# One core, hybrid encoder block with 32 experts: the last expert's part added to the stored output by an indirect DMA, experts 30 and 31 in turn, down weights issued in order of use

## The chip, the cores and the metric

One NeuronCore of a Trainium2 chip runs the whole program. Five engines work side by side, each on its own list of instructions, and meet only at semaphores: PE (matmul), DVE (VectorE), ACT (ScalarE), POOL (GpSimd) and SP (SyncE, which here does nothing but issue DMAs). Sixteen DMA engines move data; the DMAs that SP issues form one queue, those of ACT and of POOL others. The metric is the device time of one execution in microseconds (us), smaller is better. It holds a little more than the span of the profile: for the profiled execution of the kernel before, 1085.68 us against a span of 1083.8 us.

## What is computed

512 tokens of width 1024 go through one layer: two attention-like branches, their mixing, and then a mixture of 32 experts with 8 per group. The change lies wholly in the experts' part:

```python
def hier_moe(h, w_rg, b_rg, w_re, b_re, w_gate, w_up, w_down):
    """Top-1 expert group, then top-2 SwiGLU experts inside that group."""
    ...
    gates = jnp.einsum('tk,tke->te', top_w, jax.nn.one_hot(expert_ids, N_EXPERTS, dtype=f32))
    y = jnp.zeros((B * S, D), f32)
    for e in range(N_EXPERTS):
        hid = jax.nn.silu(t @ w_gate[e]) * (t @ w_up[e])
        y = y + gates[:, e:e + 1] * (hid @ w_down[e]).astype(f32)
    return y.reshape(B, S, D)
...
        x = x + hier_moe(h2, ...).astype(dt)
    return x
```

All inputs and the output are float32. Each token goes to two experts, so that an expert has 32 tokens on average.

## The kernel before

The kernel gives every expert 48 slots in a block of 64 rows (`SLOTS`, `WIDE`), and two experts share the 128 partitions as a pair. The pair's tokens are gathered from DRAM by an indirect DMA on POOL's queue (L2254), transposed on PE (L1093) and evicted by DVE. Should an expert have more than 48 tokens, a loop behind the last expert runs once more for each further block; in the runs here it has no round (`n_more` is 0), though every engine loads `n_more` and branches over the loop.

**One expert on PE.** `product(e)` multiplies with the gate and up weights (L1106, 32 matmuls, two pieces of 2 MB), ACT applies SiLU (L1510), DVE multiplies with the up half into `hid` (L2021), PE transposes it (L1112), ACT copies the result into `hidT` (L1514), and `down_of(e)` multiplies with the down weights (L1122, 16 matmuls, one piece of 2 MB). ACT (L1505) and DVE (L2014) split the sum `y` into a high and a low part, each fp32r. When both experts of a pair are there, `combine` brings the rows back to their tokens: for each of eight tiles of 128 tokens x 512 columns a matmul of a one-hot matrix `pick` (made by DVE, L2008) with the high part (L1128) and one with the low part (L1129), after which DVE adds the tile to `x2` (L1996). The eight tiles of a pair are spread over the next two experts, four each, with three PSUM banks in rotation, so that a tile waits until DVE has added the one three tiles before it.

**Weights.** All expert weights come by SP's queue, in the order that SP issues them. Gate and up pieces, numbered u = 2e and 2e + 1 (W60 and W61 are those of expert 30, W62 and W63 those of expert 31), go round through a ring of seven places, the down pieces (D30 is that of expert 30; D31 comes in two halves) through three. SP waits until PE has freed a place and issues the next load into it. In the loop over e it issues W(2e+1), W(2e+2) and then D(e), although the order of use is W(2e), W(2e+1), D(e), W(2e+2).

**The end.** PE runs `product(30)`, four tiles of pair 14, the transposes, `product(31)`, four tiles, the transposes, and then both down products one behind the other (L1122, 32 matmuls). Expert 31 has banks of its own (4 and 7) and its own `hidT_last`, so that nothing waits between the two. Then `combine_last` makes the eight tiles of the last pair. For two of them PE first copies `x2` into the bank by a matmul with the identity (L1149), and ACT evicts and stores them (L1559, L1561); the other six DVE adds (L1996), and SP stores each as it is done (L630). The last instructions (L118) are the meeting of all engines at the program's end.

Of the kernel before, what the change touches and what calls it, by code (L numbers as in the profile page):

```python
# [64 lines left out]
def encoder_block(nc, x, norm1_g, w_in, gla_w_a2, gla_b_a, gla_norm_g, dsa_q_norm_g, dsa_k_norm_g,  # L65
# [38 lines left out]
    outd = out[0].rearrange("(t p) d -> p t d", p=P)  # L104
    wind = w_in[0].rearrange("(k p) n -> p k n", p=P)
# [12 lines left out]
    with ExitStack() as ctx:  # L118
# [120 lines left out]
        def product_bank(e):  # L239
            return bank[{1: 6, NE - 1: 4}.get(e, 0)]  # L240

        def y_bank(e):
            return bank[{1: 3, NE - 1: 7}.get(e, 1)]
# [4 lines left out]
        def up_half(e):  # L248
# [10 lines left out]
        m_pick = [piece_r(0, 512, 512 * hf) for hf in range(2)]  # L259
# [16 lines left out]
        hidT, hidT_last = [columns.rearrange("p (c h s) -> p c h s", c=2, h=2)  # L276
                           for columns in (bias[3][:, 256:512], piece(5, words=256))]

        def hidT_of(e):
            return hidT_last if e == NE - 1 else hidT  # L280

# [48 lines left out]
        tok_more = sb("tok_more", [P, 2])  # L330
# [13 lines left out]
            m_w m_idx m_xg m_pick m_comb m_added wdn_last  # L344
# [81 lines left out]
        COPIED = {3: 0, TILES - 1: 4}  # L426
        ADDED = [j for j in range(TILES) if j not in COPIED]

        def last_added(j):

            return TILES * (PAIRS_E - 1) + ADDED.index(j) + 1

# [11 lines left out]
        def combined_in(e):  # L444


            p, q = divmod(e, 2)
            if p == 0:
                return [], []
            tiles = list(range(TILES * (p - 1), TILES * p))[T * q:T * q + T]  # L450
            ahead = 3 if q and e < NE - 1 else 4
            return tiles[:ahead], tiles[ahead:]
# [26 lines left out]
        def _(sp):  # L479
# [113 lines left out]
            for e in range(4, NE):  # L593
                sp.wait_ge(s["gu_part"], e)
                load(2 * e + 1)
                if e < NE - 1:
                    sp.wait_ge(s["gu_ready"], e - 2)
                    load(2 * e + 2)
# [3 lines left out]
                if e < NE - 2:  # L602
                    sp.wait_ge(s["y_ready"], e - 2)
                    if e == 4:
                        load_down_half(4, 0)
                    else:
                        load_down(e)
# [19 lines left out]
            for j in ADDED:  # L627
                hf, t = divmod(j, T)
                sp.wait_ge(s["x_added"], last_added(j))
                sp.dma_start(outd[:, t, hf * BLK:(hf + 1) * BLK], x2[:, t, hf * BLK:(hf + 1) * BLK])\  # L630
                    .then_inc(s["out_stored"], 16)
# [4 lines left out]
        def _(pe):  # L636
# [506 lines left out]
            def combine_last():  # L1143

                p = PAIRS_E - 1
                pe.wait_ge(s["x_added"], TILES * p)
                for j, b in COPIED.items():
                    hf, t = divmod(j, T)
                    mm(bank[b][:, :], ident[:, :], x2[:, t, hf * BLK:(hf + 1) * BLK], start=True, stop=False)  # L1149
                for j in range(TILES):  # L1150
                    hf, t = divmod(j, T)
                    if t == 0:
                        pe.wait_ge(s["pick_ready"], 2 * p + hf + 1)
                        pe.wait_ge(s["y_lo_ready"], 4 * p + 4 if hf else 4 * p + 3)
                    b = COPIED[j] if j in COPIED else COMB_BANKS[ADDED.index(j) % 3]
                    if j not in COPIED and ADDED.index(j) >= 3:
                        pe.wait_ge(s["x_added"], last_added(ADDED[ADDED.index(j) - 3]))
                    cols = slice(t * P, (t + 1) * P)
                    mm(bank[b][:, :], pick[hf][:, cols], y_hi[p % 2][hf], start=j not in COPIED, stop=False)
                    mm(bank[b][:, :], pick[hf][:, cols], y_lo[p % 2][hf], start=False, stop=True)\  # L1160
                        .then_inc(s["comb_ps"], 1)
# [17 lines left out]
            def down_of(e):  # L1179
# [4 lines left out]
                down(y_bank(e), [wdn_half(e, h) for h in range(2)], e % 2, s["y_ready"], hidT_of(e),  # L1184
# [18 lines left out]
            for e in (NE - 2, NE - 1):  # L1203
                front, _ = combined_in(e)
                product(e)
                combine(front)
                if e == NE - 1:
                    pe.wait_ge(s["hidT_ready"], e)
                transposes_of(e)
            down_of(NE - 2)  # L1210
            down_of(NE - 1)

            n_more = pe.value_load(own_i[0:1, MORE:MORE + 1], min_val=0, max_val=MORE)
            with pe.If(n_more > 0):
                pe.wait_ge(s["x_added"], TILES * (PAIRS_E - 1))
                pe.wait_ge(s["y_lo_ready"], 2 * NE)
                with pe.Fori(0, n_more) as t:
# [7 lines left out]
                    pe.wait_ge(s["hidT_ready"], t + (NE + 1))  # L1225
                    down(bank[1], [wdn[0][:, h] for h in range(2)], 0, s["y_ready"])
                    pe.wait_ge(s["y_lo_ready"], t * 2 + (2 * NE + 2))
                    pe.wait_ge(s["m_pick"], t * 2 + 2)
                    for j in range(TILES):
                        hf, i = divmod(j, T)  # L1230
                        if j >= 3:
                            pe.wait_ge(s["m_added"], t * TILES + (j - 2))
                        combine_tile(bank[COMB_BANKS[j % 3]][:, :], m_pick[hf], y_hi[0][hf], y_lo[0][hf], i, s["m_comb"])
                    pe.wait_ge(s["m_added"], t * TILES + TILES)
            combine_last()
# [3 lines left out]
        def _(act):  # L1239
# [272 lines left out]
            def evict_hidT(e):  # L1512
                act.wait_ge(s["hidT_ps"], e + 1)
                A(hidT_of(e), bank[5][:, 0:HALF].rearrange("p (c h s) -> p c h s", c=2, h=2), ACT.Copy)\  # L1514
# [16 lines left out]
            for e in (NE - 2, NE - 1):  # L1531
                silu(e)
                evict_hidT(e)
            for e in (NE - 2, NE - 1):
                evict_y(e)

            n_more = act.value_load(own_i[0:1, MORE:MORE + 1], min_val=0, max_val=MORE)
            with act.If(n_more > 0):
                act.wait_ge(s["comb_ps"], TILES * (PAIRS_E - 1))
                with act.Fori(0, n_more) as t:  # L1540
# [12 lines left out]
                    high_parts(bank[1], 0, 0, s["y_hi_ready"])  # L1553


            for i, (j, b) in enumerate(COPIED.items()):
                hf, t = divmod(j, T)
                act.wait_ge(s["comb_ps"], TILES * (PAIRS_E - 1) + j + 1)
                A(x2[:, t, hf * BLK:(hf + 1) * BLK], bank[b][:, :], ACT.Copy).then_inc(s["act_s"], 1)  # L1559
                act.wait_ge(s["act_s"], 2 * T + i + 1)  # L1560
                act.dma_start(outd[:, t, hf * BLK:(hf + 1) * BLK], x2[:, t, hf * BLK:(hf + 1) * BLK])\  # L1561
                    .then_inc(s["out_stored"], 16)
            act.wait_ge(s["out_stored"], 16 * TILES)


        @block.vector
        def _(dve):
# [377 lines left out]
            st.did(V.memset(tok_more[:, :], float(S)))  # L1945
# [71 lines left out]
            def gated(e):  # L2017
                dve.wait_ge(s["silu_ready"], e + 1)
                if e in (1, NE - 1):
# [16 lines left out]
            pick_tokens(0)  # L2036
            for e in range(2, NE - 2):
# [12 lines left out]
            for e in (NE - 2, NE - 1):  # L2050
                front, _ = combined_in(e)
                add_combined(front[:1])
                gated(e)
                add_combined(front[1:])
# [272 lines left out]
```

## Time and profile before

| | us |
|---|---|
| median of 3 runs | 1085.6 |
| lowest and highest | 1085.42 and 1088.79 |
| profiled execution | 1085.68 |
| its span | 1083.8 |
| granted TensorE clock, mean | 0.997 of full speed |

| engine | busy us | share of the span |
|---|---|---|
| PE | 1056.9 | 98% |
| DVE | 545.2 | 50% |
| ACT | 343.6 | 32% |
| POOL | 290.4 | 27% |

The experts take the span from about 634 us on. PE's busy share cannot say by itself what bounds this stretch, since the DMA engines are as full as PE is. Two things tell more: the chain of work that ended last, with the stretches in which PE waits for something the profile does not name ("issue"), and the time from each DMA's issue to its landing, which gives the moment at which each piece of weights is there. The stretch behind the last weight is read from the timeline.

### The profile page before, as it was taken

What the parts mean: (1) busy time and instruction counts of PE and PEld (TensorE: products, weight loads), DVE (VectorE), ACT (ScalarE), POOL (GpSimd) and SP (SyncE); (2) the same over time, 40 slices, a digit from 0 to 9 for tenths busy, and PEclk for the clock granted to TensorE, in tenths of its full rate; (3) what the DMA queues carried; (4) which work ended last, traced back from release to release, by engine and by line L of the source; (5) the groups of instructions that cost most, each with busy time, mean ns of one, the idle gap of its engine ahead of it and who ended that gap; (6) DMA issues with size and microseconds to landing.
All of it is one profiled execution on the core that took longest, in us unless ns stands there. A gap on an engine that the chain in (4) does not pass through costs nothing.

```text
span 1083.8 us, 13000 instructions
## 1 busy us (share of the span) xinstructions
PE 1056.9 (98%) x5078; PEld 689.7 (64%) x5078; DVE 545.2 (50%) x1030; ACT 343.6 (32%) x620; POOL 290.4 (27%) x197
## 2 busy tenths in 40 slices
PE   7999999999999999999999999999999999998998
PEld 6777888777788888888888853444444444443443
DVE  4533895699850432239993363333333333333334
ACT  6356632445442555541233311111111111111111
POOL 6733344455552544443423010000000000000000
PEclk9999999999999999999999999999999999999999
DMA  8613333224051322244459989999999999999995
GB/s 214 162 40 78 78 78 78 60 78 117 21 141 37 75 78 59 59 161 133 115 195 380 330 348 426 425 428 426 425 428 426 427 427 425 425 426 429 428 427 209
DMA packets 117598, 263.39 MB, mean 243 GB/s; under 512 B 11808, under 2 KB 97824, under 8 KB 104224
## 3 DMA queue, kind: packets, MB, share of 16 engines
q1 hardware_dynamic: 113792, 255.75, 63.0%
q0 software_dynamic: 2352, 4.18, 1.1%
q10 hardware_dynamic: 1392, 2.62, 0.6%
q8 instruction: 41, 0.67, 0.3%
q14 instruction: 21, 0.17, 0.0%
HBM read 262.33 MB, written 4.20 MB: 246 GB/s over the span
## 4 chain that ended last, share of the span: by engine, by line
PE 95%; issue 2%; DMA 1%; DVE 1%; ACT 0%; SPq 0%; DVEq 0%; ACTq 0%
PE bank L1106 20%; PE bank L653 19%; PE bank L672 14%; PE bank L1122 11%; PE bank L908 8%; PE bank L999 4%; PE bank L1128 3%; PE bank L1129 2%; PE bank L880 2%; PE bank L863 2%; PE bank L1093 1%; PE bank L1112 1%; PE bank L871 1%; PE bank L748 1%; PE bank L810 1%
## 5 line engine op out<-in xcount | busy, mean ns | idle before, releaser
L2138 POOL TENSOR_TENSOR piece_r<-arena,piece_r 128x1024 fp32r<-128x1024 f32 x84 | 203.0, 2424 | 240.5 <-ACT piece_r L1267 240.2
L1106 PE MATMUL bank<-arena,work 128*64 128x512 f32 x1024 | 225.5, 592 | 0.0
L653 PE MATMUL bank<-piece_r 128*128 128x512 f32 (+1 forms) x936 | 218.6, 389 | 0.0
L653 PEld LDWEIGHTS bank<-piece_r 128*128 128x128 f32 x936 | 172.5, 188 | 35.9 <-issue 3.5
L1106 PEld LDWEIGHTS bank<-arena,work 128*64 128x64 f32 x1024 | 77.5, 137 | 140.6 <-issue 140.5
L1996 DVE TENSOR_TENSOR arena<-bank,arena 128x512 f32<-128x512 f32 x126 | 81.9, 683 | 165.4 <-PE bank L1129 165.0
L672 PE MATMUL bank<-piece_r 128*128 128x512 f32 x672 | 155.9, 391 | 0.5 <-ACT piece_r L1267 0.5
L672 PEld LDWEIGHTS bank<-piece_r 128*128 128x128 f32 x672 | 125.3, 188 | 29.2 <-issue 3.5
L1267 ACT ACTIVATE piece_r<-arena 128x1024 fp32r<-128x1024 f32 x83 | 87.5, 1058 | 97.3 <-DMA arena<-w_branch_gla_in 49.8
L2254 POOL DMA_INDIRECT arena<-x_rows,idx_pair x15 | 15.2, 1010 | 329.4 <-PE bank L1093 313.6
L2014 DVE TENSOR_TENSOR piece_r<-bank,piece_r 64x512 fp32r<-64x512 f32 x64 | 44.1, 688 | 98.5 <-ACT piece_r L1505 97.5
L908 PE MATMUL bank<-piece_r 128*128 128x512 f32 x384 | 87.6, 390 | 0.0
L1122 PE MATMUL bank<-arena,bias 128*64 128x512 f32 x336 | 78.6, 609 | 6.9 <-issue 6.8
L908 PEld LDWEIGHTS bank<-piece_r 128*128 128x128 f32 x384 | 72.0, 188 | 14.9
L1505 ACT ACTIVATE piece_r<-bank 64x512 fp32r<-64x512 f32 x64 | 37.8, 591 | 134.5 <-PE bank L1122 133.7
L1510 ACT ACTIVATE bias<-bank,slot_sc 128x256 f32<-128x256 f32 x32 | 15.2, 474 | 173.1 <-PE bank L1106 171.0
L1757 DVE CUSTOM_DVE_ANT_0 work<-bank,bias 128x128 f32<-128x128 f32 (+3 forms) x32 | 15.7, 491 | 106.3 <-PE bank L863 105.4
L1694 DVE RECIPROCAL work<-work 128x512 f32<-128x512 f32 x16 | 53.6, 3347 | 3.0 <-ACT work L1359 3.0
L1122 PEld LDWEIGHTS bank<-arena,bias 128*64 128x64 f32 x336 | 23.6, 139 | 48.8 <-issue 44.4
L1783 DVE RECIPROCAL arena<-arena 128x512 f32<-128x512 f32 x16 | 53.6, 3353 | 0.5
L1128 PE MATMUL bank<-piece_r 128*128 128x512 f32 x120 | 53.2, 443 | 0.0
L1129 PE MATMUL bank<-piece_r 128*128 128x512 f32 x120 | 47.4, 395 | 0.0
(278 smaller groups left out, 1123.4 us busy)
## 6 DMA issues: line engine op xcount, KB each, us to landing
arena<-w_exp_gu_in SPq DMA_DIRECT2D x57, 2048.0 KB, 29.4
arena<-w_exp_down_in SPq DMA_DIRECT2D x18, 2048.0 KB, 29.8
arena<-w_in_in SPq DMA_DIRECT2D x68, 512.0 KB, 4.7
wdn_spare<-w_exp_down_in SPq DMA_DIRECT2D x8, 2048.0 KB, 30.2
arena<-w_exp_gu_first_in SPq DMA_DIRECT2D x4, 2048.0 KB, 11.8
arena<-w_exp_gu_in SPq DMA_DIRECT2D x6, 1024.0 KB, 7.7
arena<-w_exp_down_in SPq DMA_DIRECT2D x5, 1024.0 KB, 8.6
wdn_spare<-w_exp_down_in SPq DMA_DIRECT2D x5, 1024.0 KB, 12.6
```

Source lines behind the costliest of these rows:

```text
L653: last = mm(bank[n % 2][:, cols], w[:, k, :], h[:, k, cols], start=(i == 0 and k == 0), stop=(i == 2 and k == K - 1))
L672: last = mm(bank[n % 2][:, :], h[:, k, t * P:(t + 1) * P], w[:, :, k, :], start=(w is hi and h is hT_hi and k == 0), stop=(w is lo and k = ...
L908: last = mm(bank[2 * (f % 2) + 1 - i][:, :], w[:, k, :], h[:, k, :], start=(part == 0 and k == 0), stop=(part == 2 and k == K - 1))
L1106: last = mm(onto[hf * WIDE:(hf + 1) * WIDE, :], hTe[q][:, k, :], both[2 * k // K][:, k % (K // 2), :, hf * HALF:(hf + 1) * HALF], start=(k ...
L1122: last = mm(onto[half * WIDE:(half + 1) * WIDE, :], hidT[:, k % 2, k // 2, :], halves[k // 2][:, k % 2, hf * 512:(hf + 1) * 512], start=(k ...
L1128: mm(onto, picked[:, t * P:(t + 1) * P], hi, start=True, stop=False)
L1129: mm(onto, picked[:, t * P:(t + 1) * P], lo, start=False, stop=True).then_inc(done, 1)
L1267: A(quarter(w_hi, q), quarter(w_raw, q), ACT.Copy).then_inc(s["whi_ready"], 1)
L1694: st.did(V.reciprocal(rms[j % 2], rms[j % 2]))
L1783: st.did(V.reciprocal(gates[g][:, f], gates[g][:, f]))
L1996: return V.tensor_tensor(x2[:, t, hf * BLK:(hf + 1) * BLK], picture, x2[:, t, hf * BLK:(hf + 1) * BLK], ALU.add)
L2138: Q.tensor_tensor(quarter(w_lo, q), quarter(w_raw, q), quarter(w_hi, q).bitcast(F32), ALU.subtract).then_inc(s["wlo_ready"], 1)
```

## The change

**The end of PE's work.** Expert 30 is finished (product, transposes, down product) before expert 31 is begun. Then the last four tiles of pair 14 and `product(31)` run. The eight tiles of the last pair are then combined with expert 30's rows alone: four ahead of expert 31's transposes, four behind them, over five banks (`LAST_BANKS`). Only then comes `down_of(31)`. DVE adds all eight tiles, SP stores them, and the copies by the identity matmul, ACT's two evictions and ACT's two stores are gone.

**Expert 31.** ACT copies its down product as it stands into `last_y` (128 x 512, one instruction). POOL waits until all eight stores have landed and until `last_y` is ready, and then issues an indirect DMA that adds the rows of `last_y` to the half rows of the output in DRAM whose numbers stand in `add_rows`; rows of empty slots have a number past the end and are left out. POOL waits for its landing, and only then loads `n_more`.

**Indices.** After pair 0 DVE computes `add_rows` from `tok_pair` (two instructions on 64 x 1) and overwrites expert 31's entries in `tok_pair` (two memsets of 64 x 1), so that `pick` of the last pair names expert 30's tokens only.

**Weights.** From e = 16 on SP issues W(2e+1), D(e), W(2e+2), which is the order of use. D(e) still waits for the down product of expert e - 3, and W(2e+2) now stands behind that wait. In the experts before 16 nothing changes.

```diff
             for e in range(4, NE):
                 sp.wait_ge(s["gu_part"], e)
                 load(2 * e + 1)
+                if e >= DOWN_AHEAD and e < NE - 1:
+                    sp.wait_ge(s["y_ready"], e - 2)
+                    load_down(e)
                 if e < NE - 1:
                     sp.wait_ge(s["gu_ready"], e - 2)
                     load(2 * e + 2)
...
-            sp.wait_ge(s["y_ready"], NE - 4)
-            load_down(NE - 2)
             sp.wait_ge(s["y_ready"], NE - 3)
             load_down_half(NE - 1, 0)
             sp.dma_start(wdn_half(NE - 1, 1), wdd[NE - 1][:, 1]).then_inc(s["wdn_last"], 16)
+
+            for j in range(TILES):
+                hf, t = divmod(j, T)
+                sp.wait_ge(s["x_added"], last_added(j))
+                sp.dma_start(outd[:, t, hf * BLK:(hf + 1) * BLK], x2[:, t, hf * BLK:(hf + 1) * BLK])\
+                    .then_inc(s["out_stored"], 16)
...
-            for e in (NE - 2, NE - 1):
-                front, _ = combined_in(e)
-                product(e)
-                combine(front)
-                if e == NE - 1:
-                    pe.wait_ge(s["hidT_ready"], e)
-                transposes_of(e)
+            front, _ = combined_in(NE - 2)
+            product(NE - 2)
+            combine(front)
+            transposes_of(NE - 2)
             down_of(NE - 2)
+            front, back = combined_in(NE - 1)
+            combine(front + back)
+            product(NE - 1)
+            pe.wait_ge(s["x_added"], TILES * (PAIRS_E - 1))
+            combine_last(range(T))
+            transposes_of(NE - 1)
+            combine_last(range(T, TILES))
             down_of(NE - 1)
...
-            combine_last()
...
+            act.wait_ge(s["y_ready"], NE)
+            A(last_y, bank[1][:, :], ACT.Copy).then_inc(s["last_y"], 1)
...
+            front, back = combined_in(NE - 1)
+            add_combined(front[:1])
+            low_parts(NE - 2)
+            add_combined(front[1:] + back)
             pick_tokens(PAIRS_E - 1)
-            for e in (NE - 2, NE - 1):
-                low_parts(e)
+            gated(NE - 1)
+            for j in range(TILES):
+                dve.wait_ge(s["comb_ps"], last_added(j))
+                add_tile(j, bank[LAST_BANKS[j % len(LAST_BANKS)]][:, :]).then_inc(s["x_added"], 1)
...
+            def add_to_rows(n):
+                pool.wait_ge(s["add_rows_ready"], 2 * n)
+                pool.wait_ge(s["last_y"], n)
+                pool.indirect_dma_start(
+                    out=out_half_rows, out_offset=bass.IndirectOffsetOnAxis(ap=add_rows[:, 0:1], axis=0),
+                    in_=last_y, in_offset=None, bounds_check=2 * S - 1, oob_is_err=False,
+                    compute_op=ALU.add).then_inc(s["rows_added"], 16)
+                pool.wait_ge(s["rows_added"], 16 * n)
+
+            pool.wait_ge(s["out_stored"], 16 * TILES)
+            add_to_rows(1)
             pool.wait_ge(s["own_ready"], 1)
```

SP's queue at the end of the weights. The rows on w_exp_gu_in are W pieces, those on w_exp_down_in D pieces; x2 or x3 are pieces in a row. Before:

```order
97 L542 DMA arena<-w_exp_down_in 128x4096
98 L559 DMA arena<-w_exp_gu_in 128x4096 x2
99 L542 DMA wdn_spare<-w_exp_down_in 128x4096
100 L559 DMA arena<-w_exp_gu_in 128x4096 x2
101 L542 DMA arena<-w_exp_down_in 128x4096
102 L559 DMA arena<-w_exp_gu_in 128x4096 x3
103 L542 DMA arena<-w_exp_down_in 128x4096
104 L545 DMA wdn_spare<-w_exp_down_in 128x2048
105 L612 DMA wdn_spare<-w_exp_down_in 128x2048
```

After:

```order
99 L537 DMA wdn_spare<-w_exp_down_in 128x4096
100 L554 DMA arena<-w_exp_gu_in 128x4096 x2
101 L537 DMA arena<-w_exp_down_in 128x4096
102 L554 DMA arena<-w_exp_gu_in 128x4096 x2
103 L537 DMA arena<-w_exp_down_in 128x4096
104 L554 DMA arena<-w_exp_gu_in 128x4096 x2
105 L540 DMA wdn_spare<-w_exp_down_in 128x2048
106 L607 DMA wdn_spare<-w_exp_down_in 128x2048
107 L612 DMA out_rows<-arena 128x512 x8
```

Three W pieces in a row (W61, W62, W63, ahead of D30) have become W60 and W61, then D30, then W62 and W63; the stores now come from one place in SP's list, all eight.

PE from expert 31's product on. Before (L1106 is the product, L1112 the transposes, L1122 the down products, of both experts in a row; the tiles, L1128 and L1129, are left out):

```order
576 L1106 MATMUL bank<-arena,work 64x512 x16
...
585 L1112 MATMUL bank<-ident,bias 128x128 x2
586 L1122 MATMUL bank<-arena,bias 64x512 x8
587 L1122 MATMUL bank<-wdn_spare,arena 64x512 x8
...
626 L1149 MATMUL bank<-arena,ident 128x512 x2
```

After (L1102 is the product, L1108 the transposes, L1118 the down product, L1124 and L1125 a tile):

```order
576 L1118 MATMUL bank<-arena,bias 64x512 x8
...
585 L1102 MATMUL bank<-arena,work 64x512 x16
...
594 L1108 MATMUL bank<-ident,bias 128x128 x2
...
601 L1124 MATMUL bank<-piece_r 128x512
602 L1125 MATMUL bank<-piece_r 128x512
603 L1118 MATMUL bank<-wdn_spare,bias 64x512 x8
```

Expert 30's down product has moved ahead of expert 31's product, and the last pair's tiles ahead of expert 31's down product, which is now PE's last work.

POOL behind its last gather (L2233), after the change; before it, the load of `n_more` came at once:

```order
133 L2233 DMA arena<-x_rows,idx_pair 128x1024 [waits xg_T] x13
134 L2249 DMA out_rows<-arena,add_rows 1024x512 [waits last_y,add_rows_ready,out_stored]
135 L2258 TENSOR_LOAD own_i [waits own_ready,rows_added]
136 L2258 ISA x2
137 L2259 COMPARE_AND_BRANCH
```

The adding DMA waits for the eight stores and for `last_y`, and the load of `n_more` has come to stand behind its landing.

## Rows read from the trace of the kernel before

**Rows 1.** The page, bytes moved in each of 40 slices of 27 us.

```profile
GB/s 214 162 40 78 78 78 78 60 78 117 21 141 37 75 78 59 59 161 133 115 195 380 330 348 426 425 428 426 425 428 426 427 427 425 425 426 429 428 427 209
```

**Rows 2.** SP's issues of D29, W61, W63, half D31 (start, us), each with its landing time.

```profile
1003.62 0.33 SPq L542 DMA_DIRECT2D arena<-w_exp_down_in  x1
arena<-w_exp_down_in SPq DMA_DIRECT2D x1, 2048.0 KB, 40.3
...
1007.06 0.33 SPq L559 DMA_DIRECT2D arena<-w_exp_gu_in  x1
arena<-w_exp_gu_in SPq DMA_DIRECT2D x1, 2048.0 KB, 41.7
...
1021.75 0.33 SPq L559 DMA_DIRECT2D arena<-w_exp_gu_in  x1
arena<-w_exp_gu_in SPq DMA_DIRECT2D x1, 2048.0 KB, 36.8
...
1032.97 0.33 SPq L545 DMA_DIRECT2D wdn_spare<-w_exp_down_in  x1
wdn_spare<-w_exp_down_in SPq DMA_DIRECT2D x1, 1024.0 KB, 32.9
```

**Rows 3.** The chain that ended last, from 1042 us: start us, us, what.

```profile
1042.61 1.36 issue
1043.97 3.65 PE bank L1122 x16
1047.63 6.87 PE bank L1106 x32
1054.49 0.43 PE bank L1128
...
1056.90 7.02 PE bank L1106 x32
...
1066.34 7.02 PE bank L1122 x32
1073.35 1.91 PE bank L1149 x4
```

**Rows 4.** The timeline: start us, us, engine; then the landing of SP's output stores.

```profile
1041.10 0.48 DVE L2021 SCALAR_TENSOR_TENSOR bias<-bank,slot_sc,bias 128x256 f32<-128x256 f32 x1
1041.64 0.51 PE L1112 MATMUL bank<-ident,bias 128*128 128x128 f32 x2 [0.25 <-DVE bias L2021]
1042.18 0.38 ACT L1514 ACTIVATE bias<-bank 128x256 f32<-128x256 f32 x1 [1.86 <-PE bank L1112]
...
1075.87 3.68 DVE L1996 TENSOR_TENSOR arena<-bank,arena 128x512 f32<-128x512 f32 x6 [0.42 <-PE bank L1160]
1079.04 0.60 ACT L1559 ACTIVATE arena<-bank 128x512 f32<-128x512 f32 x1 [1.28 <-PE bank L1160]
...
DMA to landing us min/median/max: 2.1/2.9/3.7
```

**Rows 5.** POOL's last gather, all gathers' landing, a small load's, and the ends.

```profile
968.38 1.06 PE L1093 MATMUL bank<-ident,arena 128*128 128x128 f32 x8
970.21 1.00 POOL L2254 DMA_INDIRECT arena<-x_rows,idx_pair  x1 [30.11 <-PE bank L1093]
DMA to landing us min/median/max: 8.5/10.4/10.6
...
27.86 0.50 POOL L2176 DMA_DIRECT2D arena<-gla_b_a_in  x1
DMA to landing us min/median/max: 1.8/1.8/1.8
...
L2267 POOLq TENSOR_LOAD <-own_i x1: 503/503/503, 970.0 to 970.0; - x1
...
L118 POOLq DRAIN  x1: 10345/10345/10345, 971.3 to 971.3; - x1
...
L118 SPq DRAIN  x1: 13/13/13, 1083.6 to 1083.6; - x1
```

More of the change, by code:

```diff
@@ L258, in encoder_block @@
         pick = [piece_r(11, 512, at) for at in (3584, 1024)]
-        m_pick = [piece_r(0, 512, 512 * hf) for hf in range(2)]
+        last_y = piece(0, words=512)
         m_scratch = piece(0, words=D, off=1024)
@@ L275, in encoder_block @@
         hid = bias[3][:, 0:256]
[L276 to L280, printed above, removed]
+        hidT = bias[3][:, 256:512].rearrange("p (c h s) -> p c h s", c=2, h=2)
         tok_iota = sb("tok_iota", [P, S])[:, :]
@@ L424, in encoder_block @@
         COMB_BANKS = (2, 3, 6)
-        COPIED = {3: 0, TILES - 1: 4}
-        ADDED = [j for j in range(TILES) if j not in COPIED]
+        LAST_BANKS = (2, 3, 6, 4, 7)
         def last_added(j):
-            return TILES * (PAIRS_E - 1) + ADDED.index(j) + 1
+            return TILES * (PAIRS_E - 1) + j + 1
+        DOWN_AHEAD = NE // 2
         LOTS = {5: 2, R: 2, R + 1: 2}
@@ L625, in _ @@
                         .then_inc(s["m_w"], 16)
[L627 to L631, printed above, removed]
             sp.wait_ge(s["out_stored"], 16 * TILES)
@@ L1141, in combine, with combine_last @@
                     combine_tile(bank[COMB_BANKS[c % 3]][:, :], pick[hf], y_hi[p % 2][hf], y_lo[p % 2][hf], t, s["comb_ps"])
-            def combine_last():
+            def combine_last(tiles):
                 p = PAIRS_E - 1
[L1146 to L1150, printed above, removed]
+                for j in tiles:
                     hf, t = divmod(j, T)
@@ L1153, in combine_last @@
                         pe.wait_ge(s["pick_ready"], 2 * p + hf + 1)
[L1154 to L1161, printed above, removed]
+                        pe.wait_ge(s["y_lo_ready"], 4 * p + hf + 1)
+                    if j >= len(LAST_BANKS):
+                        pe.wait_ge(s["x_added"], last_added(j - len(LAST_BANKS)))
+                    combine_tile(bank[LAST_BANKS[j % len(LAST_BANKS)]][:, :], pick[hf], y_hi[p % 2][hf], y_lo[p % 2][hf],
+                                 t, s["comb_ps"])
             def product(e):
@@ L1183, in down_of @@
                     pe.wait_ge(s["y_lo_ready"], 2 * e)
-                down(y_bank(e), [wdn_half(e, h) for h in range(2)], e % 2, s["y_ready"], hidT_of(e),
+                down(y_bank(e), [wdn_half(e, h) for h in range(2)], e % 2, s["y_ready"], hidT,
                      (s["wdn_last"], 16) if e == NE - 1 else None)
@@ L1225, in _ @@
                     pe.wait_ge(s["hidT_ready"], t + (NE + 1))
+                    pe.wait_ge(s["last_y"], t + 1)
                     down(bank[1], [wdn[0][:, h] for h in range(2)], 0, s["y_ready"])
[L1227 to L1234, printed above, removed]
-            combine_last()
         @block.scalar
@@ L1513, in evict_hidT @@
                 act.wait_ge(s["hidT_ps"], e + 1)
-                A(hidT_of(e), bank[5][:, 0:HALF].rearrange("p (c h s) -> p c h s", c=2, h=2), ACT.Copy)\
+                A(hidT, bank[5][:, 0:HALF].rearrange("p (c h s) -> p c h s", c=2, h=2), ACT.Copy)\
                     .then_inc(s["hidT_ready"], 1)
@@ L1552, in _ @@
                     act.wait_ge(s["y_ready"], t + (NE + 1))
[L1553 to L1563, printed above, removed]
+                    act.wait_ge(s["rows_added"], t * 16 + 16)
+                    A(last_y, bank[1][:, :], ACT.Copy).then_inc(s["last_y"], 1)
         @block.vector
@@ L2036, in _ @@
             pick_tokens(0)
+            odd_rows, odd_swapped = [tok_pair[rows, hf, PAIRS_E - 1:PAIRS_E]
+                                     for rows, hf in ((slice(WIDE, P), 0), (slice(0, WIDE), 1))]
+            V.tensor_scalar(add_rows[WIDE:P, :], odd_rows, 2.0, None, ALU.mult).then_inc(s["add_rows_ready"], 1)
+            V.tensor_scalar(add_rows[0:WIDE, :], odd_swapped, 2.0, 1.0, ALU.mult, ALU.add)\
+                .then_inc(s["add_rows_ready"], 1)
+            dve.wait_ge(s["add_rows_ready"], 2)
+            st.did(V.memset(odd_rows, float(S)))
+            st.did(V.memset(odd_swapped, float(S)))
+            st.settle()
             for e in range(2, NE - 2):
```

71 lines of the change are left out of this document (30 added, 41 removed).

## The prediction, made before the run

> **What bounds the kernel now.** I read the throughput by slices first. From the 25th slice on, about 650 us, the core moves 425 to 429 GB/s in every slice but the last [rows 1]: the queue of weights is full without a gap. Then I read when single pieces land, as issue plus time to landing. D29 is there at 1003.62 + 40.3 = 1043.9 us, W61 at 1007.06 + 41.7 = 1048.8, W63 at 1021.75 + 36.8 = 1058.6, the first half of D31 at 1032.97 + 32.9 = 1065.9 [rows 2]. From D29 to W61 is one piece: 4.9 us for 2 MB. The issues lie 33 to 42 us ahead of the landings, so that it is not SP that is late but the data. With 4.9 us a piece the pieces between fall at 1053.7 (W62) and 1063.4 (D30), and the second half of D31 at about 1068.3. An expert of three pieces costs the queue 14.7 us.
>
> The chain that ended last shows where this reaches PE: at 1042.61 it holds 1.36 us of "issue", and expert 29's down product starts at 1043.97, the moment at which D29 lands [rows 2, 3]. From there to the end PE has no such gap. W61 is needed in the middle of product 30, 1047.63 + 3.4 = 1051.1, and has been there for 2.2 us; W63 is needed at 1060.4 and is there at 1058.6. So the kernel is bound by the weights up to D29, and from 1043.97 on by PE's own list and what follows it: 29.4 us to the end of the last down product at 1073.35, and 10.4 us more to the end of the span [rows 3].
>
> **Order of use.** The change moves no byte in or out of the queue, and a queue that is full ends when it ended. It only exchanges neighbours. The slots stay where they are: 1034.1 W59, 1039.0 now D29, 1043.9 now W60, 1048.8 W61 as before, 1053.7 now D30, 1058.6 now W62, 1063.4 now W63, then D31 at 1065.9 and 1068.3. PE's wait for the down weights goes; what is late next is the second gate and up piece of each expert, in the middle of the product. For expert 30: PE is free of product 29 at 1034.1 + 3.4 = 1037.5, needs about 2.8 for four tiles and the transposes, and D29 is there; the down product takes 3.65, the end is at 1044.0; W60 is there; the first half of product 30 ends at 1047.4; W61 lands at 1048.8, so PE waits 1.4 us. It leaves product 30 at 1048.8 + 3.4 = 1052.2 in place of 1054.49. That is all that the order of use gives: 2.3 us, since only the last wait of a full queue counts.
>
> W(2e+2) is now issued behind the wait for expert e - 3's down product, some 7 us later than before. It then still stands behind a queue of 33 us or more, which hides it. DVE's four small instructions after pair 0 lie in a stretch where the queue of weights sets the pace; I cost them at nothing.
>
> **Experts 30 and 31 in turn.** From 1052.2, with durations of [rows 3] unless named:
>
> - four tiles of pair 14, 2.2 (1054.49 to the transposes before 1056.90): 1054.4
> - transposes of 30 and the copy to `hidT`, which nothing covers now: 1041.64 to 1042.18 + 0.38 is 0.92, with the semaphore 1.1 [rows 4]: 1055.5. D30 has been there since 1053.7
> - down product 30, half of 7.02: 1059.0
> - four tiles, 2.2, the fourth of which waits for DVE as before: 1061.2. DVE also has expert 30's low parts to do here, behind the first tile's add, so that it delays no bank
> - product 31, 6.9: 1068.1. W62 has been there since 1058.6, W63 is needed at 1064.6 and is there at 1063.4: 1.2 us to spare
> - four tiles into free banks, 2.1: 1070.2. Under them ACT makes SiLU and DVE `hid`: DVE's part ended 1.8 after product 29's end even with an add in front of it [rows 4], so that it is ready
> - transposes 0.2, four tiles 1.9, under which ACT copies `hidT`: 1072.3
> - down product 31, 3.5: 1075.8.
>
> Before, the same point was 1073.35. The eight tiles that came behind it (5.7 us with the identity copies) now lie ahead of it: PE's last work ends at 1075.8 in place of 1079.0.
>
> **The output and the add.** Two things have to be ready for the add. `last_y`: one ACT copy of 128 x 512, 0.60 [rows 4], at 1076.4. The stores: DVE is free of `hid` at about 1069.1, and adds eight tiles at 3.68 / 6 = 0.61 each [rows 4], which is slower than PE makes them, to 1074.0; the last store then lands 2.9 later (2.1 to 3.7) [rows 4], at 1077.0 (1076.2 to 1077.8). The stores are the later by 0.6. POOL's DMA starts 0.8 after its release (970.21 against the transposes' end at 969.44) [rows 5]: 1077.8.
>
> How long an adding indirect DMA takes, no row shows. The nearest from above are the gathers, 8.5 to 10.6 us, all beside a full queue of weights [rows 5], while this DMA has the queues to itself. The nearest from below is a small load of POOL's in an almost idle stretch, 1.8, of which 0.5 is issue [rows 5]. I build the value from parts: 1.0 for 128 indices as in a gather, 1.3 to read the destination (1.8 - 0.5), and 2.6 to write to DRAM (a store's 2.9 less 0.3 of issue): 4.9, which is nearer to the lower end, as an empty queue should be. It lands at 1082.7. I keep 1.8 and 10.6 for the range. A gain is excluded on this item, since nothing of this kind was there before.
>
> The Trainium skill (DMA: Bandwidth & Descriptors, Anatomy of one DMA) gives a fixed cost of about 2.0 us and the bytes over 436 GB/s for a DMA from GpSimd; 32 tokens of 4 KB would make 2.3 us, an estimate from that page, and the sum would be 2.6 us less. The same section says that most of the fixed cost is the wait for the receipt of the write, heaviest for HBM. That speaks against this change: store and add depend on each other, so this is paid twice in a row. The stores' 2.9 us agree with it; no row here shows the add.
>
> Behind the landing POOL still loads `n_more` and branches: from the load at 970.0 to its final wait at 971.3 is 1.3 us [rows 5]. Before, that lay far from the path. The last 0.2 us are the meeting of the engines (1083.6 to 1083.8) [rows 5].
>
> **The sum.** 1082.7 + 1.3 + 0.2 = 1084.2 us of span against 1083.8. With the 1.88 that the profiled execution has outside its span: 1086.1, against 1085.68 there and a median of 1085.6. By parts: 2.3 gained by W61's slot, 4.7 lost on PE up to the end of down product 31 (3.8 of tiles, 1.1 for `hidT`, less 0.2), and behind it 8.4 us in place of 10.4. What can be told from no change is 0.3%, 3.3 us: between 1082.3 and 1088.9.
>
> **The rivals.**
>
> - *A slow add.* The DMA reads and writes DRAM row by row and lands as late as the gathers, 10.6. For it: the only indirect DMAs in the trace take that long, and POOL's last wait of 10.3 us [rows 5] is spent on one. Against it: all of them queue beside the weights. Time 1091.8, slower than before. It decides from a landing of 7.7 us on. Chance 0.15.
> - *A quick add.* It lands like a small load, 1.8 to 3.5: 1083.0 to 1084.7, and 1082.3 or less if the stores land at their shortest too. For it: the queues are idle and 130 KB are little. Against: it has two passes over DRAM. Chance 0.17, of which 0.05 faster by over 0.3%.
> - *Waits between the engines eat more than I count.* With the two experts in turn, each handover (`hid`, `hidT`, the banks) stands bare: three or four times 0.5 us, and W63 has only 1.2 us to spare. 1087.5 to 1089. Chance 0.14, of which 0.05 slower.
> - *The reordered issue starves the queue.* SP now waits for a down product ahead of W(2e+2). If the queue ran empty once for the 7 us of the later issue, the end would move by as much: 1093. It needs a queue shorter than 7 us where 33 us stand. Chance 0.02.
> - *The order of use brings nothing at the end*, because PE is not back at W61 in time: then 1088.4 at most. Its chance is in the third case, as its price is.
>
> **How the numbers follow.** Forecast 0.49 (1085 to 1088.9), the four cases above 0.48, and 0.03 for what I don't see (0.02 faster, 0.01 slower). Faster by over 0.3%: 0.05 + 0.02 = 0.07. Slower: 0.15 + 0.05 + 0.02 + 0.01 = 0.23. Within 0.3%: 0.70. The range goes from the quick add, 1083.0, to just short of the slow one's end, 1091.5; less than 0.2 is left out.
>
> **What would show it.** In the profile after: "issue" ahead of the down products (L1118) gone and about 1 us in the middle of each late product (L1102) in its place; W61 landing at about 1048.8; the last down product ending at 1075.8; eight adds of DVE in a row to 1074; the add starting at 1077.8, with the last store as its releaser, not `last_y`; POOL's load of `n_more` about 1.3 us before the end. The forecast is wrong if the landing of the add lies outside 3.5 to 7.6 us, if a piece of weights lands at another time than the slots say, or if PE shows gaps behind product 30.

## The result

| | us |
|---|---|
| before, median of 6 runs on the same chip | 1086.41 |
| after, median of 6 runs (1089.73 to 1091.21) | 1090.84 |
| after / before | 1.004, 95% interval 1.003 to 1.0049 |
| profiled execution after, its span | 1089.4 |

The kernel is slower by 4.4 us. The time lies in the range of the prediction, but 4.7 us over its value, and on the side that had a chance of 0.23. The chain that ended last, from the last wait for weights on (start us, us, what):

```profile
1006.72 42.98 DMA arena<-w_exp_gu_in
1049.71 0.04 issue
1049.75 3.65 PE bank L1102 x16
...
1055.85 0.39 ACT bias L1498
1056.25 0.04 issue
1056.29 3.65 PE bank L1118 x16
...
1062.12 7.04 PE bank L1102 x32
...
1070.18 3.58 DVE arena L1971 x6
...
1074.98 4.45 DMA out_rows<-arena
...
1080.28 1.65 POOL out_rows L2249
```

W61 (the first row) lands at 1049.7, PE waits for it in the middle of product 30, and then goes through without a gap but for the 0.47 us for `hidT`. That answers [rows 3], where the last wait stood ahead of expert 29's down product. DVE's adds end at 1074.97, the last store lands at 1079.43, and the add starts at 1080.28. From 800 us on the wait of PE has changed its name: it was 9.2 us in 7 pieces ahead of the down products (listed as "issue"), and is now, in the list of waits (us in total, times, longest),

```profile
PE bank L1102 <- DMA arena<-w_exp_gu_in: 6.5, 6, 2.5
...
PE bank L1118 <- ACT bias L1498: 0.5, 1, 0.5
```

Last, the end. The eight stores by their line (L612), which answers [rows 4], and the add in the list of DMAs (us to landing):

```profile
DMA to landing us min/median/max: 2.1/2.4/4.4
```

```profile
out_rows<-arena,add_rows POOLq DMA_INDIRECT x1, 3.5
```

Behind it, instruction by instruction (duration in ns, start in us): L2258 and L2259 are POOL's load of `n_more` and its branch, L119 the meeting of the engines. It answers [rows 5]:

```profile
L2258 POOLq TENSOR_LOAD <-own_i x1: 510/510/510, 1083.8 to 1083.8; - x1
...
L2259 POOLq COMPARE_BRANCH  x1: 53/53/53, 1084.7 to 1084.7; - x1
...
L119 POOLq DRAIN  x1: 1862/1862/1862, 1087.3 to 1087.3; - x1
...
L119 SPq DRAIN  x1: 13/13/13, 1079.6 to 1079.6; - x1
```

The add has landed at 1083.8. The program ends at 1089.4, 5.6 us later, in which no engine computes: 0.9 us to load and branch, 2.6 us until POOL begins its final wait (DRAIN), 1.9 us in it, 0.2 us to meet. SP's and ACT's final waits take 0.01 us.

Forecast and measurement, step by step:

| | forecast | measured | error of this step |
|---|---|---|---|
| W61 lands | 1048.8 | 1049.7 | +0.9 |
| last down product ends | 1075.8 | 1076.8 | +0.1 |
| DVE's last add ends | 1074.0 | 1075.0 | +0.1 |
| last store has landed | 1077.0 | 1079.4 | +1.5 |
| adding DMA starts | 1077.8 | 1080.3 | 0.0 |
| add has landed | 1082.7 | 1083.8 | -1.4 |
| POOL's final wait begins | 1084.0 | 1087.3 | +2.2 |
| span | 1084.2 | 1089.4 | +1.9 |

(The third column takes each step from the measured step ahead of it; the down product is not on the path.) It adds up to 5.2 us. Two questions stay for experiments: what the 5.6 us behind the landing are, and whether my account of the weights by slots holds, or the order of use is worth something else than I said.

### The profile page after: what moved, and what is told of

Same layout as the page of the kernel before. It is cut to its first block, busy times and chain, and to the rows that moved or that the text cites. A ratio compares the mean times of both kernels' runs of the same rounds, so it can differ in the third digit from the quotient of the medians.

```text
span 1089.4 us, 12987 instructions
## 1 busy us (share of the span) xinstructions
PE 1056.6 (97%) x5074; PEld 683.0 (63%) x5074; DVE 545.1 (50%) x1033; ACT 342.2 (31%) x617; POOL 292.3 (27%) x198
## 4 chain that ended last, share of the span: by engine, by line
PE 85%; DMA 11%; DVE 2%; issue 1%; ACT 1%; SPq 0%; POOL 0%; DVEq 0%; POOLq 0%; ACTq 0%
PE bank L649 18%; PE bank L1102 17%; PE bank L668 14%; PE bank L1118 8%; DMA arena<-w_exp_gu_in 8%; PE bank L904 8%; PE bank L995 4%; PE bank L1124 2%; PE bank L1125 2%; PE bank L876 2%; PE bank L859 1%; DMA arena<-w_in_in 1%; PE bank L1089 1%; PE bank L744 1%; PE bank L806 1%; PE bank L1108 1%
## 5 line engine op out<-in xcount | busy, mean ns | idle before, releaser
L1102 PE MATMUL bank<-arena,work 128*64 128x512 f32 x1024 | 228.3, 596 | 6.5 <-DMA arena<-w_exp_gu_in 6.5
L1102 PEld LDWEIGHTS bank<-arena,work 128*64 128x64 f32 x1024 | 74.0, 138 | 153.5 <-issue 140.0
L668 PE MATMUL bank<-piece_r 128*128 128x512 f32 x672 | 155.9, 391 | 0.6 <-ACT piece_r L1251 0.6
L2233 POOL DMA_INDIRECT arena<-x_rows,idx_pair x15 | 15.1, 1004 | 326.2 <-PE bank L1089 310.4
L904 PE MATMUL bank<-piece_r 128*128 128x512 f32 x384 | 87.6, 390 | 0.0
L1118 PE MATMUL bank<-arena,bias 128*64 128x512 f32 x336 | 76.9, 598 | 0.6 <-ACT bias L1498 0.5
L1124 PE MATMUL bank<-piece_r 128*128 128x512 f32 x128 | 56.5, 441 | 0.0
L1125 PE MATMUL bank<-piece_r 128*128 128x512 f32 x128 | 50.5, 395 | 0.0
L1118 PEld LDWEIGHTS bank<-arena,bias 128*64 128x64 f32 x336 | 22.2, 136 | 42.4 <-issue 36.0
```

Source lines behind the costliest of these rows:

```text
L668: last = mm(bank[n % 2][:, :], h[:, k, t * P:(t + 1) * P], w[:, :, k, :], start=(w is hi and h is hT_hi and k == 0), stop=(w is lo and k = ...
L904: last = mm(bank[2 * (f % 2) + 1 - i][:, :], w[:, k, :], h[:, k, :], start=(part == 0 and k == 0), stop=(part == 2 and k == K - 1))
L1102: last = mm(onto[hf * WIDE:(hf + 1) * WIDE, :], hTe[q][:, k, :], both[2 * k // K][:, k % (K // 2), :, hf * HALF:(hf + 1) * HALF], start=(k ...
L1118: last = mm(onto[half * WIDE:(half + 1) * WIDE, :], hidT[:, k % 2, k // 2, :], halves[k // 2][:, k % 2, hf * 512:(hf + 1) * 512], start=(k ...
L1124: mm(onto, picked[:, t * P:(t + 1) * P], hi, start=True, stop=False)
L1125: mm(onto, picked[:, t * P:(t + 1) * P], lo, start=False, stop=True).then_inc(done, 1)
```

## Experiments: the end behind the landing

**The wait moved.** Theory 1 was that the 5.6 us are POOL's own work, theory 2 that the DMA holds POOL up. In the changed kernel POOL waits for the landing only behind the load and the branch:

```diff
                     compute_op=ALU.add).then_inc(s["rows_added"], 16)
-                pool.wait_ge(s["rows_added"], 16 * n)
...
             n_more = pool.value_load(own_i[0:1, MORE:MORE + 1], min_val=0, max_val=MORE)
             with pool.If(n_more > 0):
+                pool.wait_ge(s["rows_added"], 16)
                 pool.wait_ge(s["xg_T"], PAIRS_E)
...
                         add_to_rows(t + 2)
+                        pool.wait_ge(s["rows_added"], 16 * (t + 2))
+            pool.wait_ge(s["rows_added"], 16)
```

> The changed kernel, with POOL's wait for the landing of the add moved behind its load of n_more and the branch over the overflow part. Theory 1, the end of the changed kernel is POOL's own work behind the landing (load and branch 0.9 us, 2.6 us more until its final wait begins, 1.9 us of that wait): the first 3.5 us now run while the add is in flight, the span falls by about 3.5 us, and the final wait begins with the landing. Theory 2, POOL's final wait is held up by the DMA itself, whatever stands between: the span stays within 0.5 us.

Measured: 1086.91 us against 1086.07 for the kernel before on that chip, ratio 1.0004 (0.9995 to 1.0013). The changed kernel had a ratio of 1.004, so some 3.9 us are gone. In its trace (here L2257 is the load of `n_more`):

```profile
L2257 POOLq TENSOR_LOAD <-own_i x1: 508/508/508, 1079.5 to 1079.5; - x1
...
L2258 POOLq COMPARE_BRANCH  x1: 53/53/53, 1080.3 to 1080.3; - x1
...
L119 POOLq DRAIN  x1: 1790/1790/1790, 1083.5 to 1083.5; - x1
```

Load and branch are done at 1080.3, while the add is being issued (1079.72 to 1081.37, landing 3.6 after its start, at 1083.3); the final wait begins 0.2 us behind the landing and still takes 1.8. Theory 1 holds for 3.5 us; theory 2 falls.

**POOL without its overflow part.**

```diff
             add_to_rows(1)
-            pool.wait_ge(s["own_ready"], 1)
-            n_more = pool.value_load(own_i[0:1, MORE:MORE + 1], min_val=0, max_val=MORE)
-            with pool.If(n_more > 0):
...
```

> The changed kernel without POOL's load of n_more, its branch and the overflow part behind it (which has no round with these inputs; the other engines keep theirs). Theory 1: the 3.5 us between the landing and POOL's final wait go, as in the run with the moved wait. If the 1.9 us of the final wait are instructions being fetched, they go too, 5.4 us in all; if they belong to an indirect DMA, they stay. Theory 2: nothing changes beyond 0.5 us.

Measured: 1087.06 us, ratio 1.0007 (0.9998 to 1.0016), final wait 1783 ns. Load, branch and what follows the branch go; the final wait stays. So it is not made of instructions of this part, nor of their being fetched: from 1080 us to the end no packet of kind "instruction" moves in this trace.

**Is it the indirect DMA's, or POOL's?** Two kernels take the kernel before, which has no indirect DMA within 100 us of the end, and only let POOL be the last engine: it waits for the eight stores either ahead of its load of `n_more` (first edit) or behind the branch (second).

```diff
+            pool.wait_ge(s["out_stored"], 16 * TILES)
             pool.wait_ge(s["own_ready"], 1)
             n_more = pool.value_load(own_i[0:1, MORE:MORE + 1], min_val=0, max_val=MORE)
```

```diff
                         gather(0, row_more[:, 0:1], s["m_xg"])
+            pool.wait_ge(s["out_stored"], 16 * TILES)
```

> The kernel before, in which POOL waits for the eight stores of the output ahead of its load of n_more, so that POOL is the last engine, with no indirect DMA anywhere near. Theory P, the 5.4 us behind the landing in the changed kernel are the price of ending on POOL (load and branch 0.9, 2.6 until the final wait, 1.8 of final wait): 5 us over before. Rival Q, that price is the indirect DMA's: only the load and the branch are added, 0.9 us, and the rest is gone.

> The kernel before, in which POOL waits for the eight stores behind its load of n_more and the branch, so that only its final wait is left at the end, with no indirect DMA near. Theory P: the 1.8 us of the final wait show here too, 1.6 to 1.8 us over before. Rival Q: level with before within 0.3 us.

Measured: 1089.16 us, ratio 1.0023 (1.0013 to 1.0033), with the wait ahead; 1088.78 us, ratio 1.0019 (1.0009 to 1.0028), with the wait behind; 1086.26 us for the kernel before on that chip. Of the first kernel, the branch and the final waits, and of the second, POOL's and SP's final waits:

```profile
L2269 POOLq COMPARE_BRANCH  x1: 54/54/54, 1085.7 to 1085.7; - x1
...
L118 POOLq DRAIN  x1: 1777/1777/1777, 1086.2 to 1086.2; - x1
```

```profile
L118 SPq DRAIN  x1: 13/13/13, 1083.9 to 1083.9; - x1
...
L118 POOLq DRAIN  x1: 1706/1706/1706, 1083.9 to 1083.9; - x1
```

The final wait of POOL costs 1.7 to 1.9 us although the last indirect DMA landed 100 us ago. Theory P holds for it; what POOL would pay in a program without any indirect DMA, no run shows. The second kernel is 2.5 us over before where 1.6 to 1.8 were expected; its interval (1.0 to 3.0 us) holds both. Theory P fails for the 2.6 us: in the first kernel only 0.5 us lie between the branch (1085.7) and the final wait (1086.2), so that this kernel is 2.9 us over before and not 5.

**What the branch jumps over.** The changed kernel has 21 adds more in POOL's overflow part, over which the branch jumps. They are left out here; the add of expert 31 stays.

```diff
                         gather(0, row_more[:, 0:1], s["m_xg"])
-                        add_to_rows(t + 2)
```

> The changed kernel without the 21 adds in POOL's overflow part (the part has no round with these inputs; the add of expert 31 stays, and so do the load of n_more and the branch). The branch then jumps over a shorter list, about as long as that of the kernel before, where only 0.45 us lay between the branch and the final wait. If the 2.6 us behind the branch in the changed kernel come from the length of the list that is jumped, they fall to about 0.5, and the time by 2 us; if they come from the indirect DMA ahead of it, they stay at 2.6. Load, branch (0.9) and final wait (1.8) stay in both.

Measured: 1088.55 us against 1085.47 for before on that chip, ratio 1.0026 (1.0014 to 1.0038), in place of 1.004. L2259 is the branch:

```profile
L2259 POOLq COMPARE_BRANCH  x1: 58/58/58, 1084.2 to 1084.2; - x1
...
L119 POOLq DRAIN  x1: 1860/1860/1860, 1084.7 to 1084.7; - x1
```

0.5 us, with the same add ahead of it. The other 2.1 us came from the list that is jumped, which is 21 adds longer in the changed kernel; by the two ratios the time fell by 1.5 us, by the spans of the profiles by 2.6. The traces show instructions being fetched behind the branch (two packets of kind "instruction" in the changed kernel, one here). In the changed kernel the first of them moves at 1085.7, between the branch (1084.7) and the final wait (1087.3). Here the only one moves at 1085.3, when the final wait has begun (1084.7), and so does that of the kernel before with the wait ahead of the load (1087.1, final wait from 1086.2). That such a fetch is what POOL waits for in the changed kernel is the likely reading, but no run separates it from the length of the list, and the traces do not say whose fetch it is.

**What adding costs.** The same DMA as a plain scatter. It leaves out the addition, so that its output is not the layer's; it ran once (1090.08 us), and only its trace is used:

```diff
-                    compute_op=ALU.add).then_inc(s["rows_added"], 16)
+                    ).then_inc(s["rows_added"], 16)
```

> The changed kernel with the adding indirect DMA made a plain scatter of the same rows: the output rows of expert 31's tokens are overwritten with last_y and not added to, so that it leaves out the addition. It measures what adding costs over writing. My forecast took 1.3 us for the read of the destination and 1.0 us of issue; the add showed 1.65 us of issue and 3.5 us from start to landing. If the forecast's parts are right, the issue takes 1.0 us and the landing comes at about 2.2 us; if adding costs nothing, both stay at 1.65 and 3.5.

In the timeline (start us, us) and in the list of DMAs (us to landing):

```profile
1080.36 1.04 POOL L2249 DMA_INDIRECT out_rows<-arena,add_rows  x1 [112.16 <-DMA out_rows<-arena]
```

```profile
out_rows<-arena,add_rows POOLq DMA_INDIRECT x1, 2.3
```

Issue 1.04 us, landing 2.3 us after the start. Adding costs 0.6 us of issue and 1.2 us in all. My forecast's 1.0 for the issue fits the plain scatter, not the add (1.65), and its 1.3 for reading the destination is about all that adding costs (1.2, issue included). The error lies elsewhere: I had counted issue and write one behind the other, 3.6 us, when together they take 2.3. The estimate of 2.3 us from the Trainium skill (DMA: Bandwidth & Descriptors, Anatomy of one DMA) agrees with the plain scatter; the adding DMA is 1.2 us over it.

## Experiments: the weights

**The order of use alone.** The kernel before, with D(e) ahead of W(2e+2) from expert 16 to 30:

```diff
+                if NE // 2 <= e < NE - 1:
+                    sp.wait_ge(s["y_ready"], e - 2)
+                    load_down(e)
                 if e < NE - 1:
                     sp.wait_ge(s["gu_ready"], e - 2)
                     load(2 * e + 2)
...
-                if e < NE - 2:
+                if e < NE // 2:
...
-            sp.wait_ge(s["y_ready"], NE - 4)
-            load_down(NE - 2)
```

> The kernel before, with nothing changed but the order in which SP issues the down weights: from expert 16 on D(e) ahead of W(2e+2), up to expert 30. My account by slots of 4.9 us: product 30 ends 2.3 us earlier, but W63 now lands at 1063.4 (slot of D30) where product 31 needs it at 1058, so that PE waits 5 us there and ends its last down product 2.9 us later than before: time about 2.9 us over before. The rival, that order of use is a gain of its own (PE no longer waits for down weights): about 2.3 us under before.

Measured: 1089.33 us against 1086.07, ratio 1.0032 (1.0021 to 1.0042): 3.3 us slower. PE around product 31 (timeline, L1107):

```profile
1049.05 3.65 PE L1107 MATMUL bank<-arena,work 128*64 128x512 f32 x16 [1.11 <-DMA arena<-w_exp_gu_in]
...
1058.84 3.69 PE L1107 MATMUL bank<-arena,work 128*64 128x512 f32 x10 [3.73 <-DMA arena<-w_exp_gu_in]
```

PE leaves product 30 earlier, as reckoned, and then stands 3.73 us ahead of product 31, because W62 comes one slot later (I had put the wait at W63, one half product on; the chain has product 31 take 8.78 us in place of 7.02, so both pieces are waited for). The kernel before runs both products ahead of both down products, and there D30 ahead of W62 is not the order of use.

**The order of use where it is one.** The same up to expert 29 only; D30 stays behind W63:

```diff
+                if NE // 2 <= e < NE - 2:
+                    sp.wait_ge(s["y_ready"], e - 2)
+                    load_down(e)
...
-                if e < NE - 2:
+                if e < NE // 2:
```

> The kernel before, with D(e) ahead of W(2e+2) only for experts 16 to 29; D30 stays behind W63, which in this kernel is its order of use. By slots: product 30 ends 2.3 us earlier, W63 lands at 1058.6 and is needed at 1058.0, so that 0.6 us is lost again: the last down product ends 1.8 us earlier and the time is 1.8 us under before (0.17%). The rival, that the end hangs on the landing of D31 (1068.3): no change.

Measured: 1083.9 us against 1086.07, ratio 0.9981 (0.9972 to 0.999): 2.2 us faster (1.8 were expected), the fastest kernel of this study. The chain:

```profile
1018.36 40.17 DMA arena<-w_exp_gu_in
1058.53 0.04 issue
1058.58 3.65 PE bank L1109 x16
...
1064.65 7.02 PE bank L1125 x32
1071.67 1.91 PE bank L1152 x4
```

W63 lands at 1058.5, and the last wait for weights is now the one for it; the down products end at 1071.67 where the kernel before ended them at 1073.35 [rows 3]. The rest, 10.4 us, is as it was.

**The turn without the order.** The changed kernel with the old order up to D30 (`DOWN_AHEAD = NE - 1`):

```diff
-        DOWN_AHEAD = NE // 2
+        DOWN_AHEAD = NE - 1
```

> The changed kernel with the old order of issue: D(e) behind W(2e+2) for all experts up to 30 (W63 stays behind D30). By slots D29 lands at 1043.9 and D30 at 1058.6 (in the changed kernel 1039.0 and 1053.7). Expert 30's down product starts about 3 us later than in the changed kernel, and all behind it: 3 us over the changed kernel. The rival, that the order is worth nothing because the queue ends when it ended: within 0.5 us of the changed kernel.

Measured: 1093.65 us, ratio 1.0069 (1.0053 to 1.0084), against 1.004 of the changed kernel: 3.1 us more by the ratios, 2.6 by the spans of the two profiles. In its chain expert 30's down product (L1118) starts after "issue", the wait for D30:

```profile
1057.37 1.30 issue
1058.68 3.65 PE bank L1118 x16
```

1058.7 in place of 1056.3, 2.4 us where 3 were expected. So the changed kernel needs the new order, up to expert 30, for its own order of work.

## Experiment: a later last down product, earlier stores

The changed kernel with the moved wait, and with the last pair's first four tiles between the two halves of product 31, where PE is in any case; the other four follow it, then the transposes. DVE adds four tiles before it makes expert 31's `hid`. The edits of the moved wait, shown above, are left out here, as are those that hand the tiles down to the middle of the product.

```diff
...
-            product(NE - 1)
-            pe.wait_ge(s["x_added"], TILES * (PAIRS_E - 1))
-            combine_last(range(T))
-            transposes_of(NE - 1)
-            combine_last(range(T, TILES))
+            product(NE - 1, lambda: (pe.wait_ge(s["x_added"], TILES * (PAIRS_E - 1)), combine_last(range(T))))
+            combine_last(range(T, TILES))
+            transposes_of(NE - 1)
...
-            gated(NE - 1)
             for j in range(TILES):
+                if j == T:
+                    gated(NE - 1)
...
```

> The changed kernel with the moved wait of a1, and with the last pair's first four tiles put between the two halves of expert 31's product (the other four behind it, then the transposes). DVE's eight adds begin 3.5 us earlier and are done by about 1073, the last store lands by about 1077 where last_y is ready at 1077.5 to 1078.5 (the copy to hidT is bare now, up to 0.7 us on PE). Theory 1, the add waits for the stores and for nothing else that is later: POOL's release comes 1.3 to 2 us earlier, together with the moved wait 5 us off the changed kernel, level with before. Theory 2, the stores' landing is held up by something other than DVE's late adds: no more than a1 gives.

Measured: 1086.29 us against 1085.88, ratio 0.9999 (0.999 to 1.0008): level with before. The adds are now two groups of four, and POOL's releaser is no longer a store:

```profile
1071.90 2.47 DVE L1971 TENSOR_TENSOR arena<-bank,arena 128x512 f32<-128x512 f32 x4
...
1078.94 1.65 POOL L2250 DMA_INDIRECT out_rows<-arena,add_rows  x1 [110.50 <-ACT arena L1521]
```

and its stores, by their line:

```profile
DMA to landing us min/median/max: 2.1/2.4/2.9
```

The slowest store takes 2.9 us where it took 4.4 in the changed kernel. DVE adds a tile of 256 KB every 0.61 us, which is 430 GB/s; in the changed kernel eight come in a row, and each store lands later after its issue than the one before, from 2.1 to about 3.1 us for the seventh and 4.4 for the eighth. The throughput of the stretches of 1 us around the last of them (us, then busy time of PE, PEld, DVE, ACT, POOL, the clock, DMA share, GB/s) shows two parts:

```profile
1074.00:1075.00 1.00, 1.00 (x8) 0.33 (x6) 0.96 (x2) 0.00 (x0) 0.00 (x0) 1.00 1.03 385
1075.00:1076.00 1.00, 1.00 (x8) 0.39 (x6) 0.00 (x0) 0.00 (x0) 0.00 (x0) 1.00 1.02 367
1076.00:1077.00 1.00, 0.84 (x4) 0.00 (x0) 0.00 (x0) 0.11 (x1) 0.00 (x0) 1.00 1.05 387
1077.00:1078.00 1.00, 0.00 (x0) 0.00 (x0) 0.00 (x0) 0.49 (x1) 0.00 (x0) 1.00 0.18 57
1078.00:1079.00 1.00, 0.00 (x0) 0.00 (x0) 0.00 (x0) 0.00 (x0) 0.00 (x0) 1.00 0.06 25
```

Up to about 1077.2 the DMA engines are full, at 367 to 387 GB/s: that is the queue of the eight stores. Then the share falls to 0.06, which is one engine of sixteen, and the last store lands only at 1079.4. The other five kernels with eight stores in a row show the same tail (shares of 0.02 to 0.07), and their last store takes 4.5 to 4.9 us. The kernel before moves its eight tiles at the full rate up to 1083.0, has no tail, and its slowest store takes 3.7; nor has the kernel of this experiment a tail. So a full queue accounts for the first part of the 4.4 us only, and some 1.8 us of it, an estimate from 1077.2 + 0.4 against 1079.4, are the tail. Why a few packets lag there is not shown.

Of this kernel's gain over the one with the moved wait alone (a ratio of 0.9999 against 1.0004, within both intervals) the trace shows 0.8 us in the start of the add (1078.94 against 1079.72), less than the 1.3 I had expected at least: `last_y` has become the later of the two, as ACT's copy behind the last down product is POOL's releaser.

## Why the prediction was right or wrong

- **What bounds the kernel, and the slots.** Right. All pieces landed where the exchanged slots put them, 0.9 us later throughout (D29 at 1039.9, W60 at 1044.8, W61 at 1049.7, D30 at 1054.6). Half of the 0.9 was there before the experts began (SP's issues at 524 us lie 0.44 us later than before); runs of the same kernel differ by as much.
- **Order of use.** Right in mechanism, and about right in size. "Only the last wait of a full queue counts" fits both runs of the kernel before: 2.2 us gained where the order is one of use, 3.3 lost where it is not.
- **Experts in turn.** Right: 27.1 us from W61's landing to the end of the last down product, against 27.0 reckoned. The third rival (waits between the engines) did not come; the only gap is 0.47 us.
- **The stores.** The term "the last store then lands 2.9 later (2.1 to 3.7)" was mis-sized: 4.45. I took the middle of six stores in a kernel where the DMA engines finish together, and applied it to the last of eight in a row. In the changed kernel the engines are full until 2.2 us behind DVE's last add, and in the kernel before the last store lands 0.4 us after they fell idle: by these two the term would have been 2.6, an estimate. The rest is the tail, which nothing in the rows announced.
- **The add.** 3.5 us, at the lower end of the forecast's 3.5 to 7.6 and 1.4 below my value. The slow rival fell. Issue and write overlap, which the sum of parts had left out.
- **Behind the landing.** The step that failed. I took 1.3 us from the load to the final wait, and 0.2 for the meeting; they were 3.5 and 2.1. The rows could not give either: POOL's final wait of 10.3 us [rows 5] was read as waiting for a gather, so that its own price of 1.8 us was put at nothing, and the branch of the kernel before jumped over a shorter list, for which the 1.3 us are right (1084.9 to 1086.2 in the kernel before with the wait ahead of the load). Both had lain 100 us before the end, where nothing waits for them.
- **The verdict.** Slower by 0.4% where no difference was forecast. The gain of 2.3 us and the loss of 4.7 us on PE came as reckoned, but for the 0.9 us by which the weights were late; behind the last down product the kernel needs 12.6 us where I gave it 8.4 and the kernel before needs 10.4. That the time still lies in the range is luck: the upper end was put there for a slow add, which did not come, and the add's 1.4 us under its value hid as much of the other errors.

## What to carry to other kernels

Of a queue that is full to its end only the last wait counted here: order the pieces by the use that the engine in fact makes of them at the end. That alone made the fastest kernel of these runs. A step put at the very end of the program makes its engine the last one, and everything that this engine still does behind it, even what was free before, is on the path; for GpSimd that was 5.6 us here from the landing to the end. Loads and branches belong under the last DMA, not behind it: moved there they gave back 3.9 us. GpSimd's final wait stayed in every run.

## What the runs showed of the hardware that I had not expected

- GpSimd's final wait takes 1.7 to 1.9 us in all nine kernels in which GpSimd ends last, with or without an indirect DMA within 100 us of the end (all of them use some earlier); SP's takes 0.013 us and ACT's 0.008.
- A branch over a longer list of instructions cost GpSimd 2.6 us until its next instruction, over a shorter one 0.5 us.
- An adding indirect DMA of 128 rows of 2 KB took 1.65 us of issue and 3.5 us to landing, a plain one 1.04 and 2.3, on idle queues. It moved 0.09 MB, where 128 full rows would be 0.26: most rows are empty slots. Gathers beside a full queue of weights, without an add, took 8.5 to 10.6 [rows 5].
- Of eight stores of 256 KB in a row from SP, the last landed 4.4 to 4.9 us after its issue in all six kernels that have them, with a DMA share of about one engine of sixteen for most of the last 2 us; where the stores came in two groups of four, the slowest took 2.9.
